# A layer with token columns laid out by the host: gate products on raw columns, the norm's factor applied afterwards, the key product moved ahead

## The reference, cut to what matters

```python
h = _rmsnorm(h_res, mix_norm[l])
u = h @ w_in[l]
u_conv, q_a, k_a, v_a, q_h, f_h, i_h, g_h = _split_cols(u)
# convolution branch
a, gate = jnp.split(u, 2, axis=-1)
h = a * jax.nn.sigmoid(gate)      # then 31 causal taps per channel, LayerNorm, silu
h_res = h_res + jnp.concatenate([y_conv, y_attn, y_hgrn], axis=-1) @ w_out[l]
h_res = h_res + _hier_moe(...)
```

## Time and profile before

| | |
|---|---|
| time, 3 runs | median 521.53 us (520.95 to 523.3) |
| time of the profiled execution | 520.43 us |
| its span | 518.6 us |
| busy: PE, DVE, ACT, POOL | 481.6, 284.5, 154.6, 48.5 us |
| chain that ended last | PE 73%, DMA 14%, DVE 8% |

### The profile page before, as it was taken

One profiled execution on the slowest core, in us unless ns is written; L12 is line 12 of the kernel. 1 busy time (PEld: TensorE's weight loads), 2 busy tenths in 40 slices (PEclk: granted clock), 3 DMA queues, 4 the chain that ended last, 5 costly groups with the idle time before them and its releaser, 6 DMA issues.

```text
span 518.6 us, 11000 instructions
## 1 busy us (share of the span) xinstructions
PE 481.6 (93%) x4503; PEld 323.9 (62%) x4503; DVE 284.5 (55%) x694; ACT 154.6 (30%) x386; POOL 48.5 (9%) x58
## 2 busy tenths in 40 slices
PE   6999999999998899999999999999999999875872
PEld 5888889888786445457566556575565555444430
DVE  3787998899768855536465433243343222331267
ACT  5420257410344424322133322122222121111143
POOL 3410000000001000000110011302102111000000
PEclk9999999999998999999999999999999999998687
DMA  8991000000009799518798899999999999999974
GB/s 276 357 371 42 0 2 0 1 1 1 3 3 343 253 433 403 243 42 325 261 308 339 345 410 334 408 421 425 425 419 420 427 420 422 423 421 427 417 300 162
DMA packets 29458, 143.02 MB, mean 276 GB/s; under 512 B 4669, under 2 KB 12022, under 8 KB 20704
## 3 DMA queue, kind: packets, MB, share of 16 engines
q1 hardware_dynamic: 23360, 131.03, 63.7%
q0 software_dynamic: 5760, 10.89, 5.9%
q10 hardware_dynamic: 288, 0.39, 0.2%
HBM read 133.73 MB, written 17.30 MB: 291 GB/s over the span
## 4 chain that ended last, share of the span: by engine, by line
PE 73%; DMA 14%; DVE 8%; issue 2%; SPq 1%; ACT 1%; DVEq 0%; POOLq 0%
PE bank L1533 12%; PE bank L1871 11%; PE bank L1735 11%; DMA area_x<-in_w_exp 8%; PE bank L1879 6%; PE bank L1894 5%; PE bank L1543 4%; DMA area_g<-expert_out 3%; PE bank L1902 3%; PE bank L1473 3%; PE bank L1864 3%; PE bank L1677 2%; DMA expert_out<-area_m,cst 2%; DVE area_m L931 2%; PE bank L1751 1%
## 5 line engine op out<-in xcount | busy, mean ns | idle before, releaser
L1735 PE MATMUL bank<-area_w,area_m 128*128 128x512 f32 x128 | 56.7, 594 | 0.4 <-issue 0.4
L931 DVE SCALAR_TENSOR_TENSOR area_m<-area_g,cols,area_m 128x512 f32<-128x512 f32 x60 | 41.4, 745 | 0.0
L1735 PEld LDWEIGHTS bank<-area_w,area_m 128*128 128x128 f32 x128 | 23.6, 190 | 26.9 <-issue 26.9
L1871 PE MATMUL bank<-area_w,area_m 128*64 128x256 f32 x320 | 38.5, 383 | 1.2 <-ACT area_m L1983 1.2
L1871 PEld LDWEIGHTS bank<-area_w,area_m 128*64 128x64 f32 x320 | 22.2, 137 | 15.5 <-issue 4.0
L1871 PE MATMUL bank<-area_g,area_m 128*64 128x256 f32 x256 | 31.1, 384 | 0.0
L2096 DVE COPY cst<-bank 128x128 f32<-128x128 f32 (+1 forms) x38 | 9.9, 261 | 31.5 <-PE bank L1885 21.3
L2114 DVE COPY area_m<-bank 64x512 f32<-64x512 f32 x20 | 13.9, 694 | 21.9 <-PE bank L1894 21.9
L2105 DVE TENSOR_TENSOR cst<-cst,bank 64x128 f32<-64x128 f32 x20 | 5.9, 293 | 36.5 <-ACT cst L2021 32.8
L1879 PE MATMUL bank<-area_w,area_m 128*32 128x128 f32 x576 | 21.0, 291 | 4.8 <-DMA area_w<-in_w_exp 4.8
L1871 PEld LDWEIGHTS bank<-area_g,area_m 128*64 128x64 f32 x256 | 17.3, 136 | 11.6 <-issue 3.2
(11 more groups left out here) (443 smaller groups left out, 901.6 us busy)
## 6 DMA issues: line engine op xcount, KB each, us to landing
area_g<-in_w_exp SPq DMA_DIRECT2D x14, 2048.0 KB, 24.1
area_w<-in_w_exp SPq DMA_DIRECT2D x13, 2048.0 KB
area_w<-in_w_exp SPq DMA_DIRECT2D x16, 1024.0 KB, 23.1
area_g<-in_w_exp SPq DMA_DIRECT2D x14, 1024.0 KB, 28.4
area_x<-in_w_exp SPq DMA_DIRECT2D x4, 2048.0 KB, 20.8
area_w<-in_w_in SPq DMA_DIRECT2D x7, 1024.0 KB, 14.6
area_w<-in_w_out SPq DMA_DIRECT2D x2, 2048.0 KB, 17.2
expert_out<-area_g SPq DMA_DIRECT2D x2, 2048.0 KB, 24.7
```

The source lines that it names most:

```text
L931: ins = V.scalar_tensor_tensor(out=mixT[:, i, :], in0=src, scalar=w, in1=mixT[:, i, :], op0=ALU.mult, op1=ALU.add)
L1735: ins = T.matmul(bank[7][:, :], mixT[:, k, j * P:(j + 1) * P], w_out_sb[:, n, k, :], start=(k == 0), stop=(k == KT - 1))
L1871: ins = T.matmul(out_b[h * BC:(h + 1) * BC, 0:2 * P], x[:, k, :], w_gate_up[slot][:, :, k, h * P:(h + 1) * P], start=(k == 0), stop=(k == ...
```

## The change

The host hands in two more arrays: `turned`, the 528 tokens as columns (128 x 8 x 528), and `params`, the small parameters as columns. `x` itself is still loaded later for the residual. SP loads the gate weights in three pieces between four pieces of raw columns, each with two of the 8 tiles. DVE multiplies the gate weights by the gain (8 instructions), and PE multiplies the gate tiles from raw columns, k by k. Meanwhile ACT squares the raw tiles, DVE adds the squares (7 instructions), and PE sums them over the partitions with a matrix of ones after the sixth k. ACT makes of it the factor for all tokens (`root`), and DVE makes `hT` from the raw tiles, gain and root in 8 instructions of 128 x 528. PE takes the key tile as the `hT` tiles come. DVE then makes tw1 to tw4 and multiplies the gate products by `root` (4 instructions); ACT takes the sigmoid after that. Gone are the normalization of rows, the 33 + 8 transposes, their copies out of PSUM, and 7 fill products; three fill products on zeros open PE's work. The weight sums of a move from POOL to DVE. Those of hq to q1 move back by about a piece, into the places in which taps stood; `conv` is called for 1 tap beside hq and 4 beside hf. The taps behind hf, and beside hg and q0, are as before.

```diff
-        LOADS = [(C_GATE, 256), (C_A, 256), (C_HQ, 256), (C_HF, 256), (C_HG, 256), (C_Q, 512), (C_K, 256), (C_HI, 256)]
+        LOADS = [(C_A, 256), (C_K, 256), (C_HQ, 256), (C_HF, 256), (C_HG, 256), (C_Q, 512), (C_HI, 256)]
...
+            def gate_in(i):
+                sp.dma_start(w_in_sb[:, GATE_KS[i], C_GATE:C_GATE + 256], w_v[:, GATE_KS[i], C_GATE:C_GATE + 256]).then_inc(d_gate[i], 16)
+
+            def raw_in(i):
+                c = slice(2 * i * TT, 2 * (i + 1) * TT)
+                sp.dma_start(area_x[:, c], turned[:, c]).then_inc(d_x[i], 16)
+
+            gate_in(0)
+            raw_in(0)
+            gate_in(1)
+            raw_in(1)
+            gate_in(2)
+            raw_in(2)
+            raw_in(3)
...
+            act.dma_start(cols[:, :], params).then_inc(d_par, 16)
             act.dma_start(cst[:, 0:K_FIRST], table[:, 0:K_FIRST]).then_inc(d_cst, 16)
             act.preload_act_table_set("natural_log_exp_and_others")
+            for k in range(KT):
+                act.wait_ge(d_x[k // 2], 16)
+                nc.scalar.activation(hT[:, k, :], raw[:, k, :], ACT.Square).then_inc(squared, 1)
...
+            act.wait_ge(ss_done, 1)
+            for h in range(2):
+                step(nc.scalar.activation(root[:, half_cols(h)], bank[4 + h][:, 0:HALF], ACT.Ln, bias=eps, scale=1.0 / D))
+            nc.scalar.activation(root, root, ACT.Exp, scale=-0.5).then_inc(root_ready, 1)
+            act.preload_act_table_set("sigmoid_and_others")
+
+            def keys_out(half):
+                for g in range(2):
+                    for to in range(2):
+                        dst, s = slice(to * HD, to * HD + HD), slice(g * HD, g * HD + HD)
+                        src = half_of("k", half)[s, META * (1 - half):].rearrange("p (j t) -> p j t", j=2)
...
+            act.wait_ge(product, made("k"))
+            keys_out(0)
+            first_copy("a")
+            keys_out(1)
...
+                act.wait_ge(hT_v, KT + 5 + 2 * (i + 1))
+                nc.scalar.activation(sig[:, i, :], sig[:, i, :], ACT.Sigmoid).then_inc(evac, 1)
...
+            def gate_weights(i):
+                dve.wait_ge(d_gate[i], 16)
+                for k in range(GATE_KS[i].start, GATE_KS[i].stop):
+                    w = w_in_sb[:, k, C_GATE:C_GATE + 256]
+                    V.tensor_scalar(w, w, cols[:, 62 + k:63 + k], None, ALU.mult).then_inc(gate_w, 1)
+
+            def square_added(k):
+                dve.wait_ge(squared, k + 1)
+                if k >= 2:
+                    dve.wait_ge(sq_added, k - 1)
+                V.tensor_tensor(hT[:, 0, :], hT[:, 0, :], hT[:, k, :], ALU.add).then_inc(sq_added, 1)
...
-            weight_sums("hq")
-            weight_sums("hf")
-            weight_sums("hg", range(2))
+            dve.wait_ge(d_par, 16)
+            gate_weights(0)
+            gate_weights(1)
+            square_added(1)
+            square_added(2)
+            gate_weights(2)
+            for k in range(3, KT):
+                square_added(k)
+            weight_sums("a")
+            dve.wait_ge(root_ready, 1)
+            for k in range(KT):
+                V.scalar_tensor_tensor(out=hT[:, k, :], in0=raw[:, k, :], scalar=cols[:, 62 + k:63 + k], in1=root,
+                                       op0=ALU.mult, op1=ALU.mult).then_inc(hT_v, 1)
+
...
+            for i in range(2):
+                for h in range(2):
+                    V.tensor_tensor(sig[:, i, half_cols(h)], half_of(f"gate{i}", h), root[:, half_cols(h)], ALU.mult).then_inc(hT_v, 1)
             add_part("a", U2)
-            weight_sums("hg", range(2, 4))
+            weight_sums("hq", range(2))
             add_part("a", S15)
-            weight_sums("q0", range(2))
+            weight_sums("hq", range(2, 4))
             dve.wait_ge(evac, taken("gate1"))
             dve.wait_ge(part_made, part_count("a", P2))
             mark(V.tensor_tensor(head_of("a", 0), part_bank("a", "A")[:, 0:EDGE], sig[:, 0, 0:EDGE], ALU.mult))
-            weight_sums("q0", range(2, 3))
+            weight_sums("hf", range(2))
             add_part("a", C22)
-            weight_sums("q0", range(3, 4))
+            weight_sums("hf", range(2, 4))
             add_part("a", C12)
             dve.wait_ge(parts_added, added_count("a", C12))
             V.tensor_tensor(tail_of("a", 0), tail_of("a", 0), sig[:, 0, EDGE:], ALU.mult).then_inc(glu_done, 1)
...
             V.tensor_tensor(glu[:, 1, TAPS - 1:], glu[:, 1, TAPS - 1:], sig[:, 1, :], ALU.mult).then_inc(glu_done, 1)
             dve.wait_ge(glu_done, 2)
             dve.wait_ge(v_step, vn[0])
-            weight_sums("q1")
-            for n, taps in (("hq", (0, 0, 2, 1, 1)), ("hf", (2, 1, 2, 1, 1))):
-                for o in range(5):
-                    conv(taps[o])
-                    add_part(n, o)
+            for o in range(5):
+                conv((0, 0, 0, 0, 1)[o])
+                weight_sums("hg" if o < 2 else "q0", (range(0, 2), range(2, 4), range(0, 2), range(2, 4), ())[o])
+                add_part("hq", o)
+            for o in range(5):
+                conv((0, 0, 2, 1, 1)[o])
+                weight_sums("q1", (range(0, 2), range(2, 4), (), (), ())[o])
+                add_part("hf", o)
             conv(2)
...
+            pe.wait_ge(warm_ready, 1)
+            for _ in range(3):
+                T.matmul(bank[7][:, 0:2 * P], warm[:, 0:P], warm[:, P:3 * P], start=True, stop=True)
+            for k in range(KT):
+                pe.wait_ge(d_x[k // 2], 16)
+                pe.wait_ge(gate_w, k + 1)
+                for i in range(2):
+                    n = f"gate{i}"
+                    for h in range(2):
+                        ins = T.matmul(half_of(n, h), w_in_sb[:, k, COL[n]:COL[n] + P], raw[:, k, half_cols(h)],
+                                       start=(k == 0), stop=(k == KT - 1))
+                    if k == KT - 1:
+                        ins.then_inc(product, 1)
+                if k == KT - 3:
+                    pe.wait_ge(d_cst, 16)
+                    pe.wait_ge(sq_added, KT - 1)
+                    for h in range(2):
+                        ins = T.matmul(bank[4 + h][:, 0:HALF], cst[:, K_ONE:K_ONE + P], hT[:, 0, half_cols(h)], start=True, stop=True)
+                    ins.then_inc(ss_done, 1)
+
+            pe.wait_ge(d_win[LOAD_OF["k"]], 16)
+            for k in range(KT):
+                pe.wait_ge(hT_v, k + 1)
+                for h, t in enumerate((slice(0, cut_of("k")), slice(cut_of("k"), TT))):
+                    ins = T.matmul(half_of("k", h), w_in_sb[:, k, C_K:C_K + P], hT[:, k, t], start=(k == 0), stop=(k == KT - 1))
+            ins.then_inc(product, 1)
...
-            weight_sums("a")
             pool.wait_ge(product, 1)
...
```

More of the change, by code:

```diff
@@ L244, in trunk @@
         TT = META + SEQ
+        raw = area_x[:, :].rearrange("p (k t) -> p k t", k=KT)
+        warm = area_m[:, 0:3 * P]
+        root = area_m[:, 2 * SEQ + 2 * TT:2 * SEQ + 3 * TT]
         KW = META + P
@@ new lines, in mixer_scalar @@
+            for h in range(2):
[7 more added lines that the diff above has]
+                        src = half_of("k", half)[s, META * (1 - half):].rearrange("p (j t) -> p j t", j=2)
+                        if half == 0:
+                            meta_k = half_of("k", 0)[s, 0:META].unsqueeze(1).to_broadcast([HD, NT, META])
+                            nc.scalar.activation(kT[dst, g, :, 0:META], meta_k, ACT.Copy).then_inc(a_step, 1); an[0] += 1
+                        last = nc.scalar.activation(kT[dst, g, 2 * half:2 * half + 2, META:], src, ACT.Copy)
+                        if half == 0 and g == to == 1:
+                            last.then_inc(evac, 1)
+                        else:
+                            last.then_inc(a_step, 1); an[0] += 1
@@ L646, in mixer_scalar @@
             nc.scalar.activation(kf, kf, ACT.Exp, scale=-1.0).then_inc(kf_steps, 1)
-            act.wait_ge(product, made("k"))
-            for g in range(2):
-                for half in range(2):
-                    dst, s = slice(half * HD, half * HD + HD), slice(g * HD, g * HD + HD)
-                    meta_k = half_of("k", 0)[s, 0:META].unsqueeze(1).to_broadcast([HD, NT, META])
-                    nc.scalar.activation(kT[dst, g, :, 0:META], meta_k, ACT.Copy).then_inc(a_step, 1); an[0] += 1
-                    own = [half_of("k", h)[s, META * (1 - h):].rearrange("p (j t) -> p j t", j=2) for h in range(2)]
-                    nc.scalar.activation(kT[dst, g, 0:2, META:], own[0], ACT.Copy).then_inc(a_step, 1); an[0] += 1
-                    last = nc.scalar.activation(kT[dst, g, 2:, META:], own[1], ACT.Copy)
-                    if g == half == 1:
-                        last.then_inc(evac, 1)
-                    else:
-                        last.then_inc(a_step, 1); an[0] += 1
             act.wait_ge(b_ready, 1)
@@ L883, in weight_sum @@
                 s1, s2, s4 = (w_parts[f][:, j] for j in range(3))
-                before = 4 * (f - 1)
```

(17 more changed lines are left out.)

183 lines of the change are left out of this document (47 added, 136 removed).

## The result

| | before | after |
|---|---|---|
| median of 20 runs each | 522.59 us | 526.54 us |
| ratio, 95% interval | | 1.0076 (1.0049 to 1.0103) |
| profiled execution, its span | 520.43, 518.6 us | 529.36, 527.5 us |
| a second time: median of 29 and 13 runs | 520.86 us | 525.47 us |
| ratio, 95% interval | | 1.0053 (1.0017 to 1.0089) |

The change makes the kernel slower, by some 4 us. The medians are of all runs, the ratios leave out the slow ones (over 1.5% above the fastest of their kernel), and the second profile of the changed kernel (after_again) is of such a slow run, though its marks up to 140 us are those of the first. Single runs of one kernel differ by up to 9.4 us (before: 518.99 to 528.43 us), so the answer is read from the marks inside the profile, which repeat: the second profile has its last tap at 131.88 us against 131.92 us.

The account below looks back on a forecast made before the run. DVE's list, ending last around 134 us, was taken as the bound. Terms 0.7 - 1.2 - 2.2 + 8.0 gave +5.3 us, so 525.7 us on the profiled run, 526.8 us on the median; forecast 526.3 us, range 522.8 to 529.0 us.

Parts of the forecast that it names:

- sum at the centring: At DVE's centring behind the states: 0.7 - 1.2 - 2.2 + 8.0 = +5.3 us, all passed on to the end.
- signs for right: Marks expected in the profile, among them piece a near 30 us, last tap near 134 us, centring's successor near 139 us.
- until piece a: Kernel start to a's first part: start at 30.6 instead of 29.90 us, key tile done, half-speed clock counted; +0.7 us.
- decays: At the decays, DVE no longer waits for ACT's exponential, since the 12 key copies move to the front; -1.2 us.
- beside hg and q0: During hg and q0, PE comes 6.4 us ahead, so DVE keeps 0.6 of its 2.8 us of waits; -2.2 us.
- run of taps: Behind q0, six taps come back uncovered, 22 tap instructions instead of 10; +8.0 us.
- slow clock at the means: Means after PE's idle 6 us: nothing in the sum; rival with late transfers 0 to 1.5 us, 528.5 us, 12%.
- rival on PE: Behind q0, PE decides: if the taps' run were covered, PE's 6.4 us lead goes through, 515 us; 6%.
- my first rival: At the front, products on zeros warm PE up: piece a near 27.8 us, sum +2.5 us, 523.8 us; 14%.
- page rule: At the front's loads, rule asking at least 512 B per transfer; `params` rows have 344 B, so the gain may come late.
- late end: Before the first gate product, transfers 1 us late give +1.7 us until piece a; gain at 6.4 us lies inside it.
- the experts swallow a shift: From 177 us, if transfers set the pace from a start that doesn't move, the delay is absorbed, 521.5 us; 9%.

Follow-up runs that it names:

- after_again: The changed kernel itself, unaltered, run and profiled once more: 525.47 us, ratio to the kernel before 1.0053.
- before_late: The kernel before with only the taps' places changed (hq 0,0,0,0,1, hf 0,0,2,1,1), six taps moved behind q0: 528.98 us, ratio 1.0151.
- drop6: The changed kernel with the last six of the convolution's 31 taps left out: 522.02 us, ratio to the kernel before 0.9966.
- no_warm: The changed kernel without its three products on zeros at PE's start: 529.29 us, ratio to the kernel before 1.0102.
- fill_gap: The changed kernel with 12 unread products put before PE's wait for the last tap: 527.26 us, ratio to the kernel before 1.0079.
- key_back: The changed kernel with the key tile, its weight load and its copies put back behind hf: 530.57 us, ratio to the kernel before 1.0125.
- old_taps: The changed kernel with the old tap places beside hq (0,0,2,1,1) and hf (2,1,2,1,1): 521.58 us, ratio to the kernel before 0.998.
- spread_taps: The changed kernel with 11 taps spread beside hq (1,1,1,1,1) and hf (1,1,2,1,1): 519.21 us, ratio to the kernel before 0.9983.
- pool_sums: The changed kernel with taps spread beside hq and hf, and q1's four weight sums on POOL instead of DVE: 520.35 us, ratio to before 0.9952.
- spread_warm: The changed kernel with taps spread beside hq and hf, and four products on zeros instead of three: 519.09 us, ratio to before 0.9955.
- pool_late: The changed kernel with taps spread, q1's weight sums on POOL only after hq's last addition: 520.47 us, ratio to the kernel before 0.9966.

## Why the prediction came out right, and where it did not

**The number** was right: 526.3 us forecast, 526.54 us measured. So were the bound (DVE's list ends last), the sign and the big term. But the sum at the centring was not: +5.3 us forecast, +2.34 us measured in the profiled pair. That the number came within 0.3 us is luck, twice: the kernel before measured 522.59 us in this comparison, 1.1 us above the 521.53 us that I added to, and the typical execution, with a slower front and a slow clock behind the centring, loses more than this pair shows there. Three of my own signs for right were missed as well: piece a near 30 us (28.48), the last tap near 134 us (131.92), the centring near 139 us (136.25).

| step | forecast | measured, profiled pair |
|---|---|---|
| until piece a | +0.7 | -1.43 |
| decays | -1.2 | -1.14 |
| beside hg and q0 | -2.2 | -3.05 |
| run of taps | +8.0 | +7.95 |
| sum at the centring | +5.3 | +2.33 |
| slow clock at the means | 0 | +0.5 |

The third row is what is left of q0's 5.62 us after the first two (`kb_ready`, in the decays, behind the wait for ACT's exponential, comes 2.57 us sooner; at the end of the decays it is 2.73 us). The fourth is 14.66 - 6.71 us.

**The run of taps** is shown from both sides: before_late adds it alone (+7.93 us), drop6 takes it away. Its +8.0 us was the sum's safest term, as it came from a count and a row. (The 60 of the prediction's rival on PE are tap instructions, two for each tap, and so are the 22.)

**Until piece a** was the term that was mis-sized. I took the three products on zeros to count for nothing, half speed for 5.5 us and 2.8 us lost. no_warm shows that this price is right for a front without them (2.7 us at the last tap). With them the loss on the 24 products is 0 us in three profiled executions, and 1.3 to 2.0 us in the other six, against 2.8 us in the sum. So I gave one value to what is a matter of the execution, and took it from beyond the slower end. By its marks the profiled pair is my first rival: piece a at 28.48 us (that rival said 27.8), the sum +2.3 us (it said +2.5). The rival's price of 523.8 us for the whole was then too low, as the end was later than its centring.

**Beside hg and q0** I left 0.6 us of DVE's 2.8 us of waits. DVE was busy 25.74 of 26 us, so nearly all of them went, and a little more than I had found as waits.

**Behind the centring** I passed the shift on and put nothing for the clock. PE's idle 5.83 us (I had said 5 to 7) brought a granted clock of 0.5 and, in this execution, +0.5 us; with fill_gap neither is there. Most of the rest of the profiled pair's 8.9 us at the end comes in steps of about 1.7 to 1.9 us: 16 products of L1712 take 8.80 us at 178.83 us and 8.66 at 243.84 us, where the kernel before took 7.10 and 6.96, and the clock falls again at 268 us, each time over a half-clock stretch of 3.4 us that the kernel before's profile does not have there. With them the shift is 6.9 us at 274 us and 6.6 us at 452 us; the last 2 us come behind that, from a cause that stays open. All three stretches also stand in the profiles of after_again, key_back, fill_gap, drop6 and before_late, two in those of no_warm, old_taps and spread_taps, one in pool_sums, none in spread_warm and pool_late. So neither PE's idle time nor the new front is needed for them: drop6 and fill_gap have no such idle time, before_late has the old front. Whether the change makes them more frequent stays open, as the kernel before was profiled once. The granted clock of the runs hardly speaks for it: its median is 0.963 for the changed kernel and 0.972 to 0.975 for the kernel before, but the 6.8 us at half speed around the means lower the mean of 527 us by 0.006 by themselves (an estimate from these two spans), and in fill_gap, without them, it was 0.972 and the time no lower. So the comparison of many runs is the better measure: 4.0 and 2.8 us by the ratios, 4.0 and 4.6 us by the medians. The profiled pair's +2.8 us behind the masked scores, and up to 1.4 us more for the slow front of most executions, come to 3 to 4 us, which is inside both intervals.

**The page rule.** The Trainium skill's rule on short rows (DMA: Bandwidth & Descriptors, Specifications) did not come to bear: 344 B rows of `params` did not hold up the first gate product. The gate weights are multiplied by the gain from 4.00 us on, and the first product starts at 5.6 to 5.8 us in nine of eleven profiled executions, at 7.20 and 7.55 us in the others; each time it is the raw piece, with long rows, that releases it. The late end that I had made of the rule, 6.4 us, was not needed. It was read from the wrong row, too: the 4 KB on POOL's queue that took 5.7 us came in rows of 512 B, which is no short row, and `params`, 43 KB, landed 2.8 us after its issue in the changed kernel.

**The other rivals.** That the experts swallow a shift is refuted by before_late (+7.93 us at the last tap, +7.65 us at the end). That PE decides behind q0 is refuted by drop6 and before_late; where ten tap instructions stand there, as in the kernel before, PE and DVE are level, and the second group of masked products waits some 0.5 us for DVE.

## What to carry to other kernels

When work is moved to make an engine's lead larger, ask which engine's list ends last at the next meeting point, and count what the move puts at its end: six taps moved out of covered places cost 8 us here, more than the 5.6 us that the new front and the moved key tile gave. Spread small pieces of work evenly between the waits, one for each, rather than in twos: that alone was worth about 1 us at 130 us against the old places, by one profile of each. And where single runs differ by 2%, compare marks along the program: a shift of 8 us is plain there, and so is the point at which it arises.

## What the runs showed of the hardware

- DVE and POOL hinder each other in SBUF. A 128x512 sum on DVE took 0.68 us alone and 1.4 to 1.8 us beside POOL's sums (pool_sums); two tap instructions in a row took 1.40 us alone and 2.41 to 3.09 us (pool_late); an addition with one operand in PSUM stayed at 0.41 us. POOL's own sums took 1.26 to 1.61 us in the kernel before and 1.4 to 1.7 us here. The Trainium skill (GPSIMD Engine Reference, 1. Specifications) says that VectorE instructions with two SBUF inputs contend with GpSimd for a shared interface. The traces agree, a tap with its scalar included.
- After 2.93 us of products on zeros and 1.3 to 3.3 us without work (1.3 to 1.6 us in all but fill_gap and pool_late), PE's real products ran at full speed in some executions (0.44 us a product from 5.6 us on) and at half in others (0.88 us, until 8.8 to 11.4 us), and a fourth product did not settle it. Without products on zeros it was half until 11.85 us.
- In all five profiles in which PE is idle for 5.83 us before the means (after, after_again, no_warm, key_back, before_late) the clock is granted at half speed for 6.8 us. It begins 2.1 to 5.1 us into the idle time, and costs 0 to 0.5 us of what stands behind. With 5.3 us of products nobody reads in the gap (fill_gap) it stayed at full speed.
